# SwiGLU column slots: from alternating high and low products to a run of high and a run of low ones

## The reference

```python
def swiglu(h, w_gate, w_up, w_down):
    return (jax.nn.silu(h @ w_gate) * (h @ w_up)) @ w_down      # 1024 -> 2816 -> 1024

p = h @ c_w_in[o]                                               # 1024 -> 3072, the short-convolution mixer "sc"
gate_b, gate_c, xt = p[..., :1024], p[..., 1024:2048], p[..., 2048:]
mix = (gate_b * causal_depthwise_conv(gate_c * xt, c_conv_w[o])) @ c_w_out[o]
```

## Time and profile before

| | |
|---|---|
| median of 3 runs | 1665.7 us (1664.59 to 1666.12) |
| profiled execution | 1665.99 us, span 1664.2 us |
| granted TensorE clock | 0.999 of full speed (2.4 GHz) |
| PE busy | 1655.0 us, 99% of the span |
| DVE, ACT busy | 1228.9 us (74%), 926.2 us (56%) |
| DMA | 358.5 MB, 215 GB/s over the span |

### The profile page before, as it was taken

The page is one execution under the profiler, slowest core; times in us unless marked ns, Lnnn a source line. Parts: engine busy times, 40 slices in busy tenths (PEclk is TensorE's granted clock), DMA queues, the critical chain, the costliest instruction groups (busy, mean ns, idle before and its releaser), DMA issues.

```text
span 1664.2 us, 22774 instructions
## 1 busy us (share of the span) xinstructions
PE 1655.0 (99%) x8740; PEld 1414.7 (85%) x8740; DVE 1228.9 (74%) x1632; ACT 926.2 (56%) x1396; POOL 153.3 (9%) x210
## 2 busy tenths in 40 slices
PE   9999999999999999999999999999999999999998
PEld 7888888888888888888899888888888889988887
DVE  6888776788888777776688876655766668986564
ACT  6655577645555455555566455554645458664553
POOL 1100100000211001020010011000002011311000
PEclk9999999999999999999999999999999999999999
DMA  8977553788859876687545557654667546357551
GB/s 300 329 268 259 166 193 102 254 287 258 284 174 332 261 251 216 248 305 259 193 167 187 168 172 265 202 187 141 230 209 253 185 134 203 110 182 239 190 189 64
DMA packets 99356, 358.47 MB, mean 215 GB/s; under 512 B 11184, under 2 KB 11696, under 8 KB 99248
## 3 DMA queue, kind: packets, MB, share of 16 engines
q1 hardware_dynamic: 92736, 334.73, 59.5%
q0 software_dynamic: 6368, 22.21, 4.4%
q10 hardware_dynamic: 144, 0.07, 0.0%
HBM read 355.85 MB, written 1.12 MB: 215 GB/s over the span
## 4 chain that ended last, share of the span: by engine, by line
PE 94%; DVE 3%; DMA 2%; ACT 1%; issue 1%; SPq 0%; DVEq 0%; POOLq 0%; POOL 0%; ACTq 0%
PE dn L548 28%; PE gu L503 19%; PE gu L537 10%; PE tp L537 10%; PE gu L536 5%; PE tp L536 5%; PE dn L518 4%; PE gu L533 1%; PE tp L533 1%; DMA raw<-in_weights 1%; PE tp L466 1%; PE dn L537 1%; PE gu L534 1%; PE tp L534 1%; PE dn L503 1%
## 5 line engine op out<-in xcount | busy, mean ns | idle before, releaser
L1784 DVE TENSOR_TENSOR w_lo<-raw,w_hi 128x1024 fp32r<-128x1024 f32 x518 | 637.3, 1241 | 216.1 <-ACT w_hi L1145 211.2
L1145 ACT ACTIVATE w_hi<-raw 128x1024 fp32r<-128x1024 f32 x520 | 547.9, 1057 | 323.9 <-PE dn L548 148.5
L503 PE MATMUL gu<-w_hi,hT 128*128 128x512 f32 x1056 | 329.0, 393 | 1.2 <-DVE w_lo L1777 0.8
L537 PE MATMUL gu<-hT,w_hi 128*128 128x512 f32 x728 | 259.5, 396 | 0.0
L537 PE MATMUL tp<-hT,w_hi 128*128 128x512 f32 x728 | 259.5, 396 | 0.0
L548 PE MATMUL dn<-w_hi,actT_hi 128*128 128x512 f32 x608 | 238.8, 393 | 0.0
L548 PE MATMUL dn<-w_lo,actT_hi 128*128 128x512 f32 x608 | 236.9, 390 | 0.0
L548 PE MATMUL dn<-w_hi,actT_lo 128*128 128x512 f32 x608 | 236.8, 389 | 0.0
L503 PEld LDWEIGHTS gu<-w_hi,hT 128*128 128x128 f32 x1056 | 195.5, 188 | 42.8 <-DVE w_lo L1784 1.6
L503 PE MATMUL gu<-w_lo,hT 128*128 128x512 f32 x528 | 205.8, 390 | 0.0
L536 PE MATMUL gu<-hT,w_lo 128*128 128x256 f32 x728 | 203.1, 279 | 0.0
(11 more groups left out here) (366 smaller groups left out, 2091.5 us busy)
## 6 DMA issues: line engine op xcount, KB each, us to landing
raw<-in_weights SPq DMA_DIRECT2D x561, 512.0 KB, 4.3
arena<-in_ada_w SPq DMA_DIRECT2D x72, 512.0 KB, 4.4
post_row<-in_post_rows POOLq DMA_DIRECT2D x10, 512.0 KB, 5.8
pre_row<-in_pre_rows POOLq DMA_DIRECT2D x10, 512.0 KB, 6.8
mod_row<-mod POOLq DMA_DIRECT2D x9, 512.0 KB, 9.2
shift_row<-mod POOLq DMA_DIRECT2D x5, 512.0 KB, 9.3
x<-in_x_in SPq DMA_DIRECT2D x4, 256.0 KB, 5.8
arena<-in_c_rows POOLq DMA_DIRECT2D x2, 512.0 KB, 8.9
```

The lines of the kernel that those rows point to most:

```text
L503: m = pe.matmul(bank, h[:, k, t * P:(t + 1) * P], w[:, r, kk * 512:(kk + 1) * 512], start=k == 0 and q == 0, stop=k == KT - 1 and q == 2)
L537: m = pe.matmul(o, w_hi[:, r, c], hT[:, :, k, :], start=False, stop=k == KT - 1)
L1145: act.activation(o, i, ACT.Copy, **kw).then_inc(done, 1)
L1784: dve.tensor_tensor(w_lo[:, r, :], raw[:, n % RAW, :], w_hi[:, r, :].bitcast(F32), ALU.subtract).then_inc(lo_ready, 1)
```

## The change

`column_slot` is replaced by `column_run`, which takes several slots and their banks. It first makes all high-weight products (8 per slot, 512 columns each), slot after slot, and then all low-weight ones (8 per slot, 256 columns each). The high run waits for a slot's high part alone (`hi_ready`); `lo_ready` is asked for at each slot's low products, and a slot is given back (`slot_used`) after its eight low products. In the FFNs a run has the step's four slots. In sc the first eight slots go alone and the other sixteen in pairs. The waits for a bank (`freed`) stand before that bank's first high product.

On ACT the up banks' copy now comes straight after slot n+1's split, with the silu behind it. On DVE the second ada sum of the step stands right behind the gate sum, ahead of one slot's split, and the up sum and the multiplication follow at once; the other four slots' splits come last.

```diff
-            def column_slot(n, o, at_half=lambda: None):
-                pe.wait_ge(lo_ready, n + 1)
-                r = n % RING
-                for k in range(KT):
...
-                    if k == 0:
-                        pe.matmul(o, w_hi[:, r, c], hT[:, :, k, :], start=True, stop=False)
-                        pe.matmul(o[:, 0:TOK], w_lo[:, r, c], hT_hi[:, k, :], start=False, stop=False)
-                    else:
-                        pe.matmul(o[:, 0:TOK], w_lo[:, r, c], hT_hi[:, k, :], start=False, stop=False)
-                        m = pe.matmul(o, w_hi[:, r, c], hT[:, :, k, :], start=False, stop=k == KT - 1)
-                m.then_inc(slot_used, 1)
+            def column_run(n, outs, freed=lambda i: None, at_half=lambda: None):
+                for i, o in enumerate(outs):
+                    freed(i)
+                    pe.wait_ge(hi_ready, n + i + 1)
+                    r = (n + i) % RING
+                    for k in range(KT):
+                        if i == 0 and k == KT // 2:
+                            at_half()
+                        pe.matmul(o, w_hi[:, r, k * P:(k + 1) * P], hT[:, :, k, :], start=k == 0, stop=False)
+                for i, o in enumerate(outs):
+                    pe.wait_ge(lo_ready, n + i + 1)
+                    r = (n + i) % RING
+                    for k in range(KT):
+                        m = pe.matmul(o[:, 0:TOK], w_lo[:, r, k * P:(k + 1) * P], hT_hi[:, k, :], start=False, stop=k == KT - 1)
+                    m.then_inc(slot_used, 1)
...
-                    for si in range(4):
+                    def bank_freed(si):
                         if j > 2 and si % 2 == 0:
                             pe.wait_ge((gate_summed, up_summed)[si // 2], COLUMN_N[s, j - 1])
                         elif si == 2:
                             pe.wait_ge(actT_lo_ready, TURN_N[s, 1, None])
                         if si == 3 and (s, j - 1) in ADA_TURN:
                             pe.wait_ge(mod_biased, 1 + ADA_TURN[s, j - 1])
-                        column_slot(n + si, column_bank(si))
+                    column_run(n, [column_bank(si) for si in range(4)], bank_freed)
...
-                for q in range(3 * KT):
+                for q in list(range(8)) + list(range(8, 3 * KT, 2)):
...
-                        column_slot(n0 + q, sc_bank(q))
+                        column_run(n0 + q, [sc_bank(p) for p in ((q, q + 1) if q >= 8 else (q,))], lambda i: bank_freed(q + i))
...
                         low_taken(j, n)
                         after_slots(n + 1, 1)
+                        low_up_taken(j, n)
                         column_gate(j)
-                        after_slots(n + 2, 1)
-                        low_up_taken(j, n)
-                        after_slots(n + 3, 3)
+                        after_slots(n + 2, 4)
...
                         gates_summed(j)
-                        after_slots(n + 1, 2)
+                        ada(j, 1)
+                        after_slots(n + 1, 1)
                         ups_summed(j)
-                        ada(j, 1)
                         column_gated(j)
-                        after_slots(n + 3, 3)
+                        after_slots(n + 2, 4)
```

More of the change, by code:

```diff
@@ L522, in col_slot @@
                 m.then_inc(slot_used, 1)
-            def column_slot(n, o, at_half=lambda: None):
-                pe.wait_ge(lo_ready, n + 1)
-                r = n % RING
-                for k in range(KT):
-                    if k == KT // 2:
-                        at_half()
-                    c = slice(k * P, (k + 1) * P)
-                    if k == 0:
-                        pe.matmul(o, w_hi[:, r, c], hT[:, :, k, :], start=True, stop=False)
-                        pe.matmul(o[:, 0:TOK], w_lo[:, r, c], hT_hi[:, k, :], start=False, stop=False)
-                    else:
-                        pe.matmul(o[:, 0:TOK], w_lo[:, r, c], hT_hi[:, k, :], start=False, stop=False)
-                        m = pe.matmul(o, w_hi[:, r, c], hT[:, :, k, :], start=False, stop=k == KT - 1)
-                m.then_inc(slot_used, 1)
+            def column_run(n, outs, freed=lambda i: None, at_half=lambda: None):
[13 more added lines that the diff above has]
+                    m.then_inc(slot_used, 1)
             def down_slot(n, acts, k, start=False, stop=False, used=True):
@@ L867, in sc, with bank_freed @@
             def sc(s, n0):
-                for q in range(3 * KT):
+                def bank_freed(q):
+                    if SC_BEFORE[q] is not None:
+                        pe.wait_ge(sc_summed, SC_BEFORE[q] + 1)
+                for q in list(range(8)) + list(range(8, 3 * KT, 2)):
                     if q == 1:
@@ L876, in sc @@
                         pe.wait_ge(state_ready, 2)
-                    if SC_BEFORE[q] is not None:
-                        pe.wait_ge(sc_summed, SC_BEFORE[q] + 1)
                     if q:
-                        column_slot(n0 + q, sc_bank(q))
+                        column_run(n0 + q, [sc_bank(p) for p in ((q, q + 1) if q >= 8 else (q,))], lambda i: bank_freed(q + i))
                     else:
                         pe.wait_ge(hT_lo_ready, 2 * TT * s + TT)
-                        column_slot(n0, sc_bank(0), lambda: pe.wait_ge(hT_lo_ready, 2 * TT * (s + 1)))
+                        column_run(n0, [sc_bank(0)], at_half=lambda: pe.wait_ge(hT_lo_ready, 2 * TT * (s + 1)))
                 out_proj(s, n0 + 3 * KT, range(KT), [[MIX0["sc"] + 1 + k // 2] * TT for k in range(KT)], apart=(0, 1))
```

## The result

The changed kernel takes 1669.05 us (median of 11 runs, 1667.48 to 1671.94) against 1665.7 us (11 runs, 1664.19 to 1666.24): a ratio of 1.0021, 95% interval 1.0014 to 1.0029. It is 3.35 us slower. That is inside the range of 1661.5 to 1670.0 and 3.25 us above the forecast of 1665.8, but the forecast had said that no change could be told, and one can: the interval leaves out 1, and the time is just past the 1669 from which I had called it slower, with a chance of 0.24. Its profiled execution took 1668.38 us with a span of 1666.6, so it shows 2.4 us of the difference.

The account below looks back on a forecast made before the run. PE was taken as the bound, 94% of the chain. 4.8 us gained in products against 4.85 us of new PE waits gave 1665.8 us in medians, no change that can be told; range 1661.5 to 1670.0.

Parts of the forecast that it names:

- The products: PE's gate and up products in unbroken runs: 4.3 us gained over 48 FFN steps and 0.5 in sc, 4.8 together.
- the bound drawn from the fast slots: Fast slots already run at the two pure rates' sum, 2.77 us; a new order wins back only slow slots' 0.04.
- Rival 2: Slow pattern returns in the runs, or the column-count rule holds: no gain, waits stay, 1670.6 us; chance 0.1.
- (a): First column step of each FFN: PE waits for the third bank, 1.0 us in ctx_ffn, 1.3 in ffn_2, none in ffn_1.
- (b): ffn_1's step 7: PE's fourth bank waits 0.3 us for the mod bias, from 0 to 3.
- The walk: Reckoning of one ffn_1 step through ACT, DVE and SP: activations' split ends 5.65 us into the next step.
- (c): ffn_1's end: DVE's later work makes PE wait 1.3 us before turning the next tile, from 0 to 2.5.
- 1.1 us of margin for the up sum: In a step of ffn_1, the up sum was to be ready 1.1 us before PE needs it: no wait.
- (d): sc's end: a later slot release delays mix tile 1, so PE waits 0.65 us, from 0 to 1.3.
- (e): ffn_2's first steps coincide with POOL's row loads and slow fetches: 0.3 us of waits, up to 3.
- Rival 3: Slots released in a bunch delay the fetch chain; PE waits at down products in ffn_1 and ffn_2: 1671.4 us; chance 0.15.
- 5.4 us of margin: In a step of ffn_1, the activations' split was to end 5.4 us before the down products want it.

Follow-up runs that it names:

- e1: Changed kernel with FFN steps in two runs of two slots and ACT and DVE in the order of before; 1663.98 us, 0.9989 to the kernel before.
- e2: Every slot by itself, 8 high then 8 low products, in FFNs and sc; ACT and DVE as in the kernel before; 1664.94 us, ratio 0.9995 to it.
- e7: Changed kernel, but ACT's four squares at the end of step 8 come behind that step's activations' split; 1667.13 us, 1.0009 to the kernel before.
- e6: Changed kernel, but each FFN's first column step in two runs of two slots; 1666.86 us, 1.0004 to the kernel before.
- e9: Changed kernel with the second input's ada sums cut to 16 of 1024 columns; 1664.81 us, 0.9996 to the kernel before.
- e3: Changed kernel's PE program, runs of four, with ACT's and DVE's order of the kernel before; 1666.50 us, 1.0006 to the kernel before.
- e4: Kernel before, with only sc done by runs as in the changed kernel; 1666.51 us, 1.0005 to the kernel before.
- e5: Changed kernel, old ACT and DVE order; FFN runs of two, four in ffn_3 to ffn_5 after the first step; sc's last four slots alone; 1663.53 us.
- e8: Kernel before, with high and low products strictly alternating in each slot; 1672.91 us, 1.0041 to the kernel before.

## Why the prediction was right, and where it was thin

**The products.** Rates from start to start, and the bound drawn from the fast slots, held: 0.2267 and 0.120 us (7.25 and 3.84 in a step). Only the end of a step was off: I took 5.45 behind 11.09 and 16.54, it is 16.553. One return to a high product costs 20 ns (e1, e2), so 3.5 us were won in the steps, not 4.3. The 0.5 us of sc's slots didn't come (73.99 and 74.00 us). Rival 2, that the order is worth nothing, is refuted by the changed kernel's steps. With it goes what the prediction drew from the Trainium skill, "TensorE: Matmul & The Clock Gate", section "Back-to-back issue gap", that the gap hangs on the column count alone: behind a low run, the first 512-column products are up to 236 ns apart where others are 227. The section gives that formula for an isolated product only.

**(a) Third banks.** Forecast 0, 1.0 and 1.3 us; 0.36, 1.02 and 0.72 came. In the changed kernel ctx_ffn's split starts at 516.14, 4.0 us into the step that begins at 512.13; before it was 4.1. So ctx_ffn's opening did repeat itself. ffn_1's split came 0.4 us later in its step than before and ffn_2's 0.6 earlier, and in e7's trace all three waits are longer. That the three sum to 2.1 where 2.3 was forecast is partly luck. Their cause is shown: e6 takes all three away.

**(b) The mod bias** at ffn_1's step 7: forecast 0.3, no gap there. The walk had the activations' split end 5.65 us into such a step; here it ended at 4.62, and the bias was ready some 0.7 us ahead of its need.

**(c) ffn_1's end.** Forecast 1.3 us at the turns; 1.16 came. Runs of two (e1) and short ada sums (e9) each take it away, so it needs both the late release and a DVE without slack, as argued. What I missed is the 1.32 us before step 10. I had reckoned 1.1 us of margin for the up sum, from a steady step, and ffn_1's steps aren't steady. In its steps 3 to 9 the split ended 9.7, 7.1, 4.65, 4.65, 4.6, 8.45 and 9.7 us in, not 5.65, and a late step makes the next one late where SP issues a fetch late for it, as at 442.41; the 4.3 us that I took for a fetch were 6.1 to 7.6 for the four issued from 422.5 to 427.2. I also had not looked at what ACT does at the end of step 8: four squares, in front of the split that the rest of DVE's list waits behind. e7 takes two thirds of the wait away, e3 (the old order of ACT and DVE) all of it.

**(d) sc's end.** Forecast 0.65 us, 0.80 came. e4 shows it apart, and in e5, where sc's last four slots go alone, it is gone.

**(e) ffn_2's fetches:** no wait at the down products, in ffn_2 or anywhere. Rival 3 did not happen, but its chain did run late: of the 5.4 us of margin 1.4 were left in ffn_1's steps 3 and 9 and 1.0 in ffn_2's step 3, behind fetches of up to 11.5 us. The cover was less than I had reckoned, and just enough.

**The sum.** 4.85 us of waits were forecast and 6.0 came; 4.8 were to be won and 3.5 to 3.7 were. Two errors of about 1.2 us with the same sign make the 2.4 us of the profiled executions, where 0.05 was forecast. Inside the waits an error is hidden: the 0.6 us of (b) and (e) didn't come, and the 1.32 us before step 10, which I had put at nothing, did. The medians are 3.35 apart. The changed kernel's runs also spread over 4.5 us, before it was 2.1; e1's spread over 1.1 and e9's over 2.7. I read this as waits that hang on when a fetch lands. e7's trace fits, with 3.7 us at the third banks where the changed kernel's has 2.1, but none of the changed kernel's longest executions was traced, so that last microsecond is argued and not shown.

## What to carry to other kernels

An edit that makes the bounding engine's own instructions cheaper is priced by start-to-start distances of the same instructions in pure runs, and these held here to 0.1% (16.54 us for a step, 16.553 measured). But what is won is a small difference of two such sums, 0.073 us a step where I had 0.09. What it asks for earlier and gives back later must be priced separately, at the places where the helping engine has least slack: first and last iterations, and iterations with side work, not the steady one. Here a middle size kept most of the gain and none of these waits: runs of two won 2.6 of the 3.5 us in products and cost nothing in the FFNs.

## What the runs showed of the hardware

Products with 512 moving columns start 227 ns apart and those with 256 start 120 apart, in the changed kernel's high runs of 32 and in the 91 of the earlier trace rows. The return from a low run to a high one costs 20 ns in sum: in the changed kernel's down products, the first high ones behind it come 233, 236, 228, 233 and 231 ns apart, and the low run's first interval is 113. With single low products between high ones, three returns cost 20 ns together (e8). Single distances differ by some ns there (232, 240 and 236 behind the three high products), so sums over a slot or a step are what to compare.
